# The order of modulation units and weight units in the shared rings of a feed-forward

## The reference, cut to what matters

```python
mod = (silu(c) @ ada_w + ada_b).reshape(B, 9, 1, 2048)      # ada_w: 2048 x 18432, c: 1 + 8 rows
sh1, sc1, gt1, sh2, sc2, gt2, sh3, sc3, gt3 = [mod[:, i] for i in range(9)]
h = rmsnorm(x, g1) * (1 + sc1) + sh1
x = x + 0.5 * gt1 * ((silu(h @ wg) * (h @ wu)) @ wd)        # wg, wu: 2048 x 5504, wd: 5504 x 2048
```

## Time and profile before

| | |
|---|---|
| median of 3 runs | 2541.29 us (2541.09 to 2541.32) |
| profiled execution, first to last instruction (span) | 2538.0 us |
| TensorE matmul busy | 2432.5 us (96%) |
| TensorE weight load busy | 2242.4 us (88%) |
| VectorE, ScalarE busy | 1241.8 us (49%), 998.4 us (39%) |
| granted clock of TensorE, mean | 0.982 |
| read from device memory | 476.53 MB, 190 GB/s over the span |

### The profile page before, as it was taken

The page is one execution under the profiler, slowest core; times in us unless marked ns, Lnnn a source line. Parts: engine busy times, 40 slices in busy tenths (PEclk is TensorE's granted clock), DMA queues, the critical chain, the costliest instruction groups (busy, mean ns, idle before and its releaser), DMA issues.

```text
span 2538.0 us, 48523 instructions
## 1 busy us (share of the span) xinstructions
PE 2432.5 (96%) x17250; PEld 2242.4 (88%) x17250; DVE 1241.8 (49%) x2324; ACT 998.4 (39%) x1523; POOL 156.0 (6%) x195
## 2 busy tenths in 40 slices
PE   5699999999999999999799999899999999999997
PEld 2378888888888888899799999799999999999997
DVE  2433433443443446655766754545344454453455
ACT  3433233233333324433456643533333333334334
POOL 3200000000000000001212211200000000000002
PEclk9799999999999999999899999899999999999999
DMA  9987777777777777754344445355555555555552
GB/s 333 371 257 241 246 245 240 244 247 242 240 245 246 241 244 245 243 164 146 102 140 141 117 125 149 98 149 157 142 155 144 148 157 142 149 156 142 155 145 79
DMA packets 704802, 480.59 MB, mean 189 GB/s; under 512 B 15349, under 2 KB 628361, under 8 KB 704377
## 3 DMA queue, kind: packets, MB, share of 16 engines
q1 hardware_dynamic: 702432, 470.74, 60.9%
q0 software_dynamic: 1776, 6.26, 0.8%
q10 hardware_dynamic: 530, 2.76, 0.3%
HBM read 476.53 MB, written 5.13 MB: 190 GB/s over the span
## 4 chain that ended last, share of the span: by engine, by line
PE 89%; DVE 4%; DMA 3%; ACT 2%; issue 1%; POOL 0%; SPq 0%; DVEq 0%; POOLq 0%; ACTq 0%
PE ps L467 28%; PE ps L469 27%; PE ps L468 27%; PE ps L480 6%; DMA raw<-in_ada_w 3%; PE ps L453 1%; DVE lo L1126 1%; DMA raw<-in_ffn_w_gate 1%; DVE h_lo L1174 1%; DVE work L1163 0%; ACT hi L824 0%; PE ps L746 0%; DVE x L1237 0%; DVE work L1374 0%; POOL work L1563 0%
## 5 line engine op out<-in xcount | busy, mean ns | idle before, releaser
L467 PE MATMUL ps<-h_hi,hi 128*128 128x320 f32 x3456 | 1095.5, 317 | 27.1 <-DVE h_lo L1174 14.7
L1126 DVE TENSOR_TENSOR lo<-raw,hi 128x1024 fp32r<-128x1024 f32 (+2 forms) x896 | 803.2, 927 | 647.3 <-ACT hi L824 640.9
L824 ACT ACTIVATE hi<-raw 128x1024 fp32r<-128x1024 f32 (+2 forms) x896 | 690.8, 803 | 1037.9 <-PE ps L469 969.4
L469 PE MATMUL ps<-h_hi,lo 128*128 128x320 f32 x3456 | 1073.0, 310 | 0.0
L468 PE MATMUL ps<-h_lo,hi 128*128 128x320 f32 x3456 | 1072.7, 310 | 0.0
L467 PEld LDWEIGHTS ps<-h_hi,hi 128*128 128x128 f32 x3456 | 653.4, 189 | 98.9 <-issue 82.8
L468 PEld LDWEIGHTS ps<-h_lo,hi 128*128 128x128 f32 x3456 | 654.2, 189 | 0.2
L469 PEld LDWEIGHTS ps<-h_hi,lo 128*128 128x128 f32 x3456 | 653.5, 189 | 0.0
L467 PE MATMUL ps<-a_hi,hi 128*128 128x320 f32 x1376 | 432.4, 314 | 1.8 <-DVE a_lo L1255 1.3
L469 PE MATMUL ps<-a_hi,lo 128*128 128x320 f32 x1376 | 425.3, 309 | 0.0
L468 PE MATMUL ps<-a_lo,hi 128*128 128x320 f32 x1376 | 425.1, 309 | 0.0
(11 more groups left out here) (193 smaller groups left out, 875.8 us busy)
## 6 DMA issues: line engine op xcount, KB each, us to landing
raw<-in_ada_w SPq DMA_DIRECT2D x288, 512.0 KB, 4.7
raw<-in_ffn_w_gate SPq DMA_DIRECT2D x172, 512.0 KB, 3.9
raw<-in_ffn_w_up SPq DMA_DIRECT2D x172, 512.0 KB, 4.0
raw<-in_ffn_w_down SPq DMA_DIRECT2D x160, 512.0 KB, 4.0
raw<-in_w_in SPq DMA_DIRECT2D x56, 512.0 KB, 3.7
raw<-in_w_out SPq DMA_DIRECT2D x32, 512.0 KB, 3.8
raw<-in_ffn_w_down SPq DMA_DIRECT2D x16, 384.0 KB, 3.0
work<-in_x_prompt ACTq DMA_DIRECT2D x2, 1024.0 KB, 11.6
```

What stands on the lines that cost most here:

```text
L467: mm(out, w_hi, r_hi, start=first, stop=False)
L469: return mm(out, w_lo, r_hi, start=False, stop=last)
L824: run(hi_slot(u)[:, 0:n], raw_slot(u)[:, 0:n], ACT.Copy).then_inc(hi_done, 1)
L1126: v.tensor_tensor(lo_slot(u)[:, 0:n], raw_slot(u)[:, 0:n], hi_slot(u)[:, 0:n], ALU.subtract).then_inc(lo_done, 1)
```

## The change

In the 28 bodies with modulation the order becomes: four modulation units, then four weight units, twice for each body. The weight units of an `up_pair` come in the order of `SIDE_BY_SIDE` (gate first half, up first half, gate second half, up second half), and TensorE runs them through `side_by_side`, as in the second feed-forward. All five engines' walks over the units follow. The rings and the distance of 4 units between the unit done and the unit split stay, so the full splits of four weight units are now made as the four modulation units ahead of them get done, and the small splits of modulation units as weight units get done.

```diff
                 def up_pair(u, turns, col, group):            # SyncE
                     for n in range(8):
-                        w, half = (SIDE_BY_SIDE if group is None else IN_TURN)[n % 4]
-                        if group is not None:
-                            mod_unit(u, turns, group, n)
-                            u += 1
+                        w, half = SIDE_BY_SIDE[n % 4]
+                        if group is not None and n % 4 == 0:
+                            for m in range(4):
+                                mod_unit(u + m, turns, group, n + m)
+                            u += 4
                         columns(u, turns, (gate, up)[w], half, col + P * (n // 4))
                         u += 1
...
                     for step in range(2):                     # TensorE
                         if group is not None:
-                            for n, (w, half) in enumerate(IN_TURN):
-                                mod_unit(u, turns, 4 * step + n, group)
-                                arrive(u + 1, turns)
-                                if half == 0:
-                                    free_bank(g + w, gturns, freed_before)
-                                for j in range(HB):
-                                    ...
-                                last.then_inc(unit_done, 1)
-                                u += 2
-                        else:
-                            for w in range(2):
-                                free_bank(g + w, gturns, freed_before)
-                            side_by_side(u, turns, (bank(g), bank(g + 1)), h0)
+                            for n in range(4):
+                                mod_unit(u + n, turns, 4 * step + n, group)
                             u += 4
+                        for w in range(2):
+                            free_bank(g + w, gturns, freed_before)
+                        side_by_side(u, turns, (bank(g), bank(g + 1)), h0)
+                        u += 4
...
-                split(u + SPLIT, None, u + SPLIT < U_F1 or u % 2 == 0)   # ScalarE and VectorE, set-up
+                split(u + SPLIT, None, True)
...
                     for n in range(8):                        # ScalarE, up_pair
-                        w, half = (IN_TURN if with_group else SIDE_BY_SIDE)[n % 4]
-                        if with_group:
-                            finished(u, turns)
-                            split(u + SPLIT, turns, not last_mod)
-                            if n == 7:
+                        if with_group and n % 4 == 0:
+                            for m in range(4):
+                                finished(u, turns)
+                                split(u + SPLIT, turns)
+                                u += 1
+                            if n == 4:
                                 copy_mod()
-                            u += 1
                         finished(u, turns)
-                        if w == 0 and half == 1:
+                        if n % 4 == 2:
                             silu(g + n // 4 * 2, n // 4)
-                        split(u + SPLIT, turns)
+                        split(u + SPLIT, turns, with_group and (n < 4 or not last_mod))
                         u += 1
...
                     for n in range(8):                        # VectorE, up_pair
-                        if group is not None:
-                            finished(u, turns)
-                            split(u + SPLIT, turns, not last_mod)
-                            u += 1
+                        if group is not None and n % 4 == 0:
+                            for m in range(4):
+                                finished(u, turns)
+                                split(u + SPLIT, turns)
+                                u += 1
                         finished(u, turns)
-                        if group is None and n % 4 == 2:
+                        if n % 4 == 2:
                             finished(u + 1, turns)
-                        if n % 4 == (2 if group is None else 3):
                             hidden(n // 4, g, gturns, first_block + n // 4, count + n // 4)
                             g += 2
                         if n == 7 and group is not None:
                             add_mod(group)
-                        split(u + SPLIT, turns)
+                        split(u + SPLIT, turns, group is not None and (n < 4 or not last_mod))
                         u += 1
```

More of the change, by code:

```diff
@@ L564, in up_pair @@
                         if group is not None:
-                            for n, (w, half) in enumerate(IN_TURN):
-                                mod_unit(u, turns, 4 * step + n, group)
-                                arrive(u + 1, turns)
-                                if half == 0:
-                                    free_bank(g + w, gturns, freed_before)
-                                for j in range(HB):
-                                    k = half * HB + j
-                                    pe.wait_ge(h_ready, h0 + k + 1)
-                                    last = products(bank(g + w), u + 1, j, P, 0, h_hi[:, k, :], h_lo[:, k, :], k == 0, k == KB - 1)
-                                last.then_inc(unit_done, 1)
-                                u += 2
-                        else:
-                            for w in range(2):
-                                free_bank(g + w, gturns, freed_before)
-                            side_by_side(u, turns, (bank(g), bank(g + 1)), h0)
+                            for n in range(4):
+                                mod_unit(u + n, turns, 4 * step + n, group)
                             u += 4
+                        for w in range(2):
+                            free_bank(g + w, gturns, freed_before)
+                        side_by_side(u, turns, (bank(g), bank(g + 1)), h0)
+                        u += 4
                         g += 2
@@ L586, in down_eight @@
                     for n in range(8):
-                        if group is not None:
-                            mod_unit(u, turns, n, group)
-                            u += 1
+                        if group is not None and n % 4 == 0:
+                            for m in range(4):
+                                mod_unit(u + m, turns, n + m, group)
+                            u += 4
                         arrive(u, turns)
@@ L911, in down_eight @@
                     for n in range(8):
-                        if with_group:
-                            finished(u, turns)
-                            if n == 7:
+                        if with_group and n % 4 == 0:
+                            for m in range(4):
+                                finished(u, turns)
+                                split(u + SPLIT, turns)
+                                u += 1
+                            if n == 4:
                                 copy_mod()
-                            split(u + SPLIT, turns, True)
-                            u += 1
                         finished(u, turns)
-                        split(u + SPLIT, turns)
+                        split(u + SPLIT, turns, with_group)
                         u += 1
@@ L1226, in _ @@
                     normed(0, 1, MOD_AT.index(u))
-                split(u + SPLIT, None, u + SPLIT < U_F1 or u % 2 == 0)
+                split(u + SPLIT, None, True)
                 if u == 8:
@@ L1275, in down_eight @@
                     for n in range(8):
[L1276 to L1279, removed]
+                        if group is not None and n % 4 == 0:
+                            for j in range(4):
+                                finished(u, turns)
+                                split(u + SPLIT, turns)
+                                u += 1
                         finished(u, turns)
@@ L1284, in down_eight @@
                             add_mod(group)
-                        split(u + SPLIT, turns)
+                        split(u + SPLIT, turns, group is not None)
                         u += 1
```

## The result

The changed kernel takes 2696.3 us (median of 4 runs, 2691.56 to 2701.38), the kernel before 2541.19 us, measured beside it. The ratio is 1.0608, with an interval of 1.0591 to 1.0625. It is 155 us slower; 2678 were forecast, between 2605 and 2725. The profiled execution has a span of 2696.9 us, 158.9 more than the 2538.0 of before.

What follows compares the result with a forecast made beforehand. TensorE, busy throughout the first feed-forward, was taken as the bound. To the span of 2538.0 us came +97 for late splits and the start, +40 for the clock, and 3.3 to the runs' median: 2678 us, range 2605 to 2725.

Steps and rivals of the forecast that it cites:

- The order and its gain: First feed-forward, TensorE: fewer switches between unit kinds save 1.0 us a block, 56 us over 56 blocks, if splits are ready.
- Rival 4: First feed-forward: splits come in time, only the fewer switches count, 56 us less, 2485 us; chance 0.03.
- S: Time from a block's first modulation unit to its first weight matmul on TensorE; 1.86 us without waiting, break-even at 2.86.
- The splits: ScalarE's copies and VectorE's subtractions for weight units come late in up and down blocks: about +100 us in all.
- VectorE's own work isn't what ends last: First block of an up body: VectorE's hidden and add_mod end 2.0 us after the block's start, before the delayed copies.
- The table load: First up blocks: ScalarE's 1.28 us activation table load waits for the first modulation unit's end, then delays the full copies.
- rival 2: First up blocks: the table load is hidden, VectorE sets the wait, about +85 us, 2626 us; chance 0.12.
- The clock: TensorE's clock falls to half behind pauses in the 20 first up blocks, 2.0 us each, 40 us in all.
- Rival 1: First feed-forward: the pauses cost no clock, which stays at 1.00; 2638 us; chance 0.20.
- rival 3: First feed-forward: both kinds of up block lose the clock, 40 falls at 2.0 us, +177, 2718 us; chance 0.13.
- The start: First body: the first weight matmul comes some 10 us later, near 123.7, but stalls shrink; taken as -3 us.
- The signs: Trace marks in the first feed-forward, such as TensorE under 85% busy, 1.5 us pauses in second blocks, clock about 0.95.

Runs made afterwards that it cites:

- e5: The changed kernel's order, with one-float splits of modulation units in a tile of their own and weight units' splits made earlier: 2498.57 us, 0.9809 of before.
- e1: The changed kernel plus a one-float Silu of ScalarE ahead of each loop of up bodies, removing the table load inside them: 2696.91 us, 1.0604 of before.
- e6: The changed kernel with e1's Silu and e3's filler matmuls together, 14 in place of 17 in first up blocks: 2643.72 us, 1.037 of before.
- e3: The changed kernel with matmuls that nobody reads filling TensorE's pauses in the first feed-forward: 2649.14 us, 1.0419 of before.
- e4: The kernel of before with two modulation units, then two weight units (MMWW), in place of one and one: 2508.37 us, 0.9867 of before.

## Why the prediction was right, step by step
**The order and its gain.** Right, to the digit: four modulation units in a row and the switch take 1.86 us (e5), the rest of a block 14.27 against 14.26, and break-even is at 2.86. Rival 4, faster, failed at the place named, the subtractions: S is 1.86 only when they begin before M0 is done.

**The splits.** Right in mechanism and nearly in size: 97.0 us for the blocks behind the first body, where the same terms make 95.5 (99.9 less the 4.4 that the first body was charged with). In the parts: first up blocks 5.57 against 5.6, second 4.46 against 4.55, last chunk 6.6 against 7.0. The first blocks of the down bodies were under-priced, 4.2 and 3.9 to 4.0 against 3.6 and 3.2. I let VectorE go from update or add_mod straight to the subtraction:

```profile
526.06 0.15 DVE L1121 TENSOR_TENSOR lo<-raw,hi 128x1 fp32r<-128x1 f32 x1
526.64 3.50 DVE L1121 TENSOR_TENSOR lo<-raw,hi 128x1024 fp32r<-128x1024 f32 x3 [0.43 <-PE ps L482]
```

Between the end of its small split (526.21) and the next one's start (526.64) lie 0.43 us which I had not counted. The trace has the branch and the register instructions of VectorE's loop there (L1286, L1292); it is where one body ends and the next begins. Behind a down body the gap is 0.60 us, and `add_mod` stands in front of it, which I had left out there. In the second blocks of up bodies the subtraction follows the small split without a gap. A gap of 0.45 us stands at the same place in e1 and, with a step to the matmul of 0.05 us and not 0.2, gives 5.12 in place of 4.85. So the step "VectorE's own work isn't what ends last" was right, but by little: the table load's chain ended 0.45 us behind it.

**The table load.** Right: it starts behind M0's end, in rows 6's way; rival 2 is out. It cost 0.26 to 0.45 us of S in a first block of chunks 1 to 4. Taking it out gained nothing in time while the clock fell (e1), and 6 us once the clock was held (e6). The Trainium skill's drain (ScalarE: Activation LUTs, What ACT_TABLE_LOAD costs) does not appear here either: the load of 443.15 ends at 444.43 and the copy starts at 444.44.

**The clock.** The mechanism is right, and this is the term whose size was most off: 55.1 us against 40. I charged 20 first blocks at 2.0 and nothing else. Behind the first body it fell in 15 of 19 of these, in 8 of 19 second blocks behind pauses of 1.27 us, and in 6 of 8 first down blocks: 29 blocks at 1.9 us. The price of one was nearly right (2.2 us in a first block, 1.5 in the others) and the places were not: shorter pauses do it too, two in a row, with modulation units between them. The second down blocks, with a single pause of 1.17 us, lost nothing. In four first blocks with the same two pauses of 0.77 and 2.62 us the clock stayed at 1.00; why there stays open. e3 shows that the pauses are the cause. Rival 1 is out, rival 3 was half true.

By the Trainium skill's rule (TensorE: Matmul & The Clock Gate, Why this matters for your kernels) pauses of 2.6 and 1.3 us would not have lowered the clock. This case's trace does not agree: in 26 of the 29 blocks no pause was longer than 2.62 us.

**The loads.** Hidden, as forecast: no idle time of TensorE in the first feed-forward ends on a DMA. The start was wrong: -3 us against a body charged with 4.4 is +1.4, and it measured +5.3. I expected the first weight matmul near 123.7. It came at 126.61, behind 7.29 us of idle time, 13.7 us later than before; by the start of the second body all but 5.3 of it had been made up.

**The signs.** TensorE was 88% busy in the first feed-forward, and not under 85%. The pause ahead of the weights was 1.27 us in the second blocks and not 1.5. The others came as named, but that behind a down body the pause among the modulation units stands between the third and the fourth.

**The sum.** 97 + 40 = 137 us on the span, measured 158.9: 15 are the clock's, 4 the start's, 1.5 the blocks', 1.7 come behind the stage. (The 40 has 2 for the first body; counted there, the clock is 17 and the start 2.) All four errors have one sign, so the 2678 does not owe its nearness to terms that cancel. The working, the forecast's case (0.50) and the range held.

## What to carry to other kernels
When two kinds of unit share a ring and only one kind needs preparing, the distance of the preparation must be read in time and not in units: at a distance of 4 units, MMWW prepares each weight unit under a weight unit, MMMMWWWW prepares it under 0.43 us modulation units. Group the cheap kind to save switches, and then check on each in-order engine when the preparation of the first unit behind the group can begin; if a kind needs no slot, give it none. Where TensorE is the bound, price a recurring pause of one to three microseconds at more than its length (here 151 us of pauses lost 55 us more to the half clock), and check the granted clock before calling a shortened wait useless: e1 shortened a wait by 0.45 us and showed nothing; with the clock held the same cut was worth 6 us.

## What the runs showed of the hardware
A switch of TensorE from full-width matmuls to those that write strips of 32 partitions and back costs about 0.34 us: a modulation unit alone takes 4.28 - 24 x 0.1465 = 0.76, one in a row 0.43. e4 gives the same (8.23 - 48 x 0.1465 - 2 x 0.43 = 0.34), and so does e5 (16.14 - 96 x 0.1465 - 4 x 0.43 = 0.36). The granted clock was lowered to half around pauses of 3.07 us (3 of 3 blocks), of 2.62 us (8 of 12), of 2.18 us (12 of 12 in e1) and, with a pause of 0.77 to 1.05 us shortly ahead, of 1.25 to 1.27 us (12 of 23), with 1.9 us lost each time in the mean of after's 29 blocks. A single pause of 1.17 us did not lower it (0 of 8). Matmuls for nothing in the pauses (21 in a first, 12 in a second up block, 6 in a down block) brought it back to 1.00 from 160 to 1150 us, and 47 us with it. An activation table load of 1.28 us ran between the end of its wait and the copy, and the copy started 0.01 us behind it. VectorE was idle for 0.43 to 0.60 us where its loop goes around, between two subtractions that stand without a gap inside a pass.
